# Closing layer 0 by token halves, with the dense branch written ahead of the sparse one

## The reference

```python
m_l = modulate(rmsnorm(h, norm2_w[l]), sh2, sc2)
h = h + g2 * grouped_moe(m_l, router_w, router_bias, ...)      # latent tokens
hc = hc + cg2 * grouped_moe(m_c, router_w, router_bias, ...)   # context tokens, other gates
...
a_l = modulate(rmsnorm(h, norm1_w[l]), sh1, sc1)               # layer 1
a_c = modulate(rmsnorm(hc, norm1_w[l]), csh1, csc1)
q_c, k_c, v_c = project(a_c)                                   # q_c is not used
q_l, k_l, v_l = project(a_l)
```

## Time and profile before

| | |
|---|---|
| median of the runs | 1494.63 us |
| the profiled execution | 1495.13 us, of which the span is 1493.3 us |
| PE busy | 1378.6 us (92% of the span) |
| DVE, ACT, POOL busy | 595.6, 393.9, 153.6 us |
| chain that ended last | PE 72%, SP's queue 10%, DMA 7%, DVE 5% |
| HBM traffic | 325.79 MB read, 14.81 MB written, 228 GB/s over the span |

### The profile page before, as it was taken

The page is one execution under the profiler, slowest core; times in us unless marked ns, Lnnn a source line. Parts: engine busy times, 40 slices in busy tenths (PEclk is TensorE's granted clock), DMA queues, the critical chain, the costliest instruction groups (busy, mean ns, idle before and its releaser), DMA issues.

```text
span 1493.3 us, 29089 instructions
## 1 busy us (share of the span) xinstructions
PE 1378.6 (92%) x12381; PEld 830.0 (56%) x12381; DVE 595.6 (40%) x1095; ACT 393.9 (26%) x970; POOL 153.6 (10%) x182
## 2 busy tenths in 40 slices
PE   5999888999988999998999999998999999998876
PEld 2344444454544588754666666656757776655432
DVE  4365666446454655451222222134264532221112
ACT  2322343443434200321222222104162302221111
POOL 0000113122231300000111111000000001111100
PEclk8999999999999999999999999999999999999998
DMA  8555334333440542416999999892220359999993
GB/s 340 215 172 175 110 138 156 126 117 138 141 142 29 137 117 97 186 59 248 324 389 379 383 380 384 344 367 81 81 104 29 130 221 392 393 394 396 398 402 144
DMA packets 131494, 334.48 MB, mean 224 GB/s; under 512 B 13283, under 2 KB 63259, under 8 KB 125211
## 3 DMA queue, kind: packets, MB, share of 16 engines
q1 hardware_dynamic: 121851, 309.18, 57.0%
q0 software_dynamic: 6208, 12.60, 2.4%
q10 hardware_dynamic: 3296, 10.73, 1.9%
HBM read 325.79 MB, written 14.81 MB: 228 GB/s over the span
## 4 chain that ended last, share of the span: by engine, by line
PE 72%; SPq 10%; DMA 7%; DVE 5%; ACT 2%; issue 2%; ACTq 0%; DVEq 0%; POOLq 0%
PE ps L1592 12%; PE ps L1234 11%; PE ps L1251 7%; SPq L587 7%; PE ps L1485 6%; PE ps L1631 6%; PE ps L1542 5%; PE ps L1178 3%; PE ps L1891 2%; SPq L589 2%; PE ps L1656 2%; PE ps L1803 2%; PE ps L1326 2%; DMA ring<-in_moe_w_down 2%; DMA ssb<-in_moe_w_up 1%
## 5 line engine op out<-in xcount | busy, mean ns | idle before, releaser
L1234 PE MATMUL ps<-aT,ring 128*128 128x512 f32 x384 | 174.8, 603 | 2.2 <-issue 2.2
L1592 PE MATMUL ps<-ring,ssb 128*32 128x256 f32 x2256 | 137.2, 387 | 9.7 <-DMA ring<-in_moe_w_up 8.9
L2415 DVE COPY big<-ps 32x256 f32<-32x256 f32 x162 | 68.6, 423 | 145.9 <-PE ps L1631 144.2
L1592 PE MATMUL ps<-tmp,ssb 128*32 128x256 f32 x1984 | 117.2, 383 | 7.2 <-DMA tmp<-in_moe_w_up 7.2
L2406 DVE TENSOR_TENSOR ssb<-ssb,ps 128x128 f32<-128x128 f32 (+1 forms) x56 | 19.1, 346 | 260.6 <-ACT ssb L1009 259.3
L1234 PEld LDWEIGHTS ps<-aT,ring 128*128 128x128 f32 x384 | 70.6, 191 | 84.8 <-issue 82.6
L1592 PEld LDWEIGHTS ps<-ring,ssb 128*32 128x32 f32 x2256 | 88.1, 112 | 53.0 <-DMA ring<-in_moe_w_up 14.3
L1251 PE MATMUL ps<-aT,ring 128*128 128x512 f32 x256 | 114.2, 595 | 0.0
L1631 PE MATMUL ps<-ring,ssb 128*32 128x256 f32 x1648 | 96.8, 387 | 3.6 <-DMA ring<-in_moe_w_down 2.9
L1592 PEld LDWEIGHTS ps<-tmp,ssb 128*32 128x32 f32 x1984 | 70.4, 111 | 50.2 <-DMA tmp<-in_moe_w_up 9.0
L1022 ACT COPY big<-ps 32x256 f32<-32x256 f32 x162 | 58.7, 363 | 141.4 <-PE ps L1631 139.9
(11 more groups left out here) (434 smaller groups left out, 1944.6 us busy)
## 6 DMA issues: line engine op xcount, KB each, us to landing
ring<-in_ada_w SPq DMA_DIRECT2D x44, 1024.0 KB
ring<-in_moe_w_down SPq DMA_DIRECT2D x40, 1024.0 KB
ring<-in_moe_w_gate SPq DMA_DIRECT2D x56, 512.0 KB
ring<-in_moe_w_up SPq DMA_DIRECT2D x56, 512.0 KB
tmp<-in_moe_w_gate SPq DMA_DIRECT2D x48, 512.0 KB
tmp<-in_moe_w_up SPq DMA_DIRECT2D x48, 512.0 KB
ring<-in_ssd_in_w SPq DMA_DIRECT2D x20, 1024.0 KB
tmp<-in_moe_w_down SPq DMA_DIRECT2D x16, 1024.0 KB
```

The source lines that it names most:

```text
L1234: ins = pe.matmul(ps[:, bank, :], slot(u)[:, k, (i % 2) * P:(i % 2 + 1) * P], aT[:, k, :], start=(k == 0), stop=(k == KD - 1))
L1592: ins = pe.matmul(tiled_gu[32 * c:32 * c + 32, 2 * h + i, :].rearrange("p (r n) -> p r n", r=2), XgT[l][:, k * C + 32 * g:k * C + 32 * g + ...
L2415: ins = dve.tensor_copy(Y[s % 2][32 * g:32 * g + 32, 256 * c:256 * c + 256], tiled_y[32 * c:32 * c + 32, 2 * h + i, :])
```

## The change

Three things are changed.

1. **The end of layer 0 by halves.** `shared_down(b)` now fills bank b with two chunks of one half (bank 0 to 3 latent, 4 to 7 context), by matmuls over 256 tokens. `layer_sum` orders PE's work: banks 0, 1, 2, 3 and 5, the first two tiles of `acc`, bank 6, the mean square of the latent half, banks 7 and 4, the last two tiles. DVE adds the latent half to `hT` (`gated_sum(0)`) between tiles 1 and 2 of `acc`, norms it behind tile 3, and then takes the context half. PE computes the latent keys (`keys(0)`), the mean square of the context half, the first query unit, the context keys (`keys(1)`), and goes on. The rotation of the keys stands behind the second query unit. The root is taken twice (`ROOTS`).
2. **The branches' order.** In PE's and DVE's programs the flag is compared with 1 (`spread`), and the dense branch stands first. The sparse branch is now reached by a jump past the dense code, and falls through into what follows. The other three engines keep `choose`.
3. **SP's queue.** In the sparse case SP waits for all four transfers of pairs before it issues layer 1's first weights. The shared down weights stay ahead of that wait.

```diff
-ROOTS = [1, 2, 1, 1]
+ROOTS = [1, 2, 2, 1]
...
+        def spread(eng, l):
+
+            eng.wait_ge(s_flag, l + 1)
+            return eng.value_load(flag[0:1, 0:1], min_val=0, max_val=1) == 1
...
+                if pairs_used:
+                    for t in range(NT if l == 0 else 0):
+                        sp_.wait_ge(s_yp[0][t], 16)
...
-            norm_modulate(1, 0, T, 0, lambda k: act.wait_ge(s_h2, k + 1))
+            act.wait_ge(s_mod, AMOD_N[1, 0])
+            for h in range(2):
+                part = slice(h * S, (h + 1) * S)
+                for k in range(KD):
+                    act.wait_ge(s_h2, 4 * h + k // 2 + 1)
+                    act.activation(aT[:, k, part], hT[:, k, part], ACT.Square).then_inc(s_sq, 1)
+                act.wait_ge(s_ms, roots_to(2) + h + 1)
+                act.activation(rstd[:, part], ps[:, h, 0:S], ACT.Sqrt, bias=small[:, 15:16]).then_inc(s_rs, 1)
+                for k in range(KD):
+                    act.wait_ge(s_nx, parts_to(2) + KD * h + k + 1)
+                    act.activation(aT[:, k, part], aT[:, k, part], ACT.Identity, bias=mod[:, 1, k, h:h + 1],
+                                   scale=amod[:, 1, 0, k, h:h + 1]).then_inc(s_a, 1)
...
+            def mean_square_half(h):
+                for k in range(KD):
+                    pe.wait_ge(s_sq, squares_to(2) + KD * h + k + 1)
+                    ins = pe.matmul(ps[:, h, 0:S], mean[:, :], aT[:, k, h * S:(h + 1) * S], start=(k == 0), stop=(k == KD - 1))
+                ins.then_inc(s_ms, 1)
...
-                def shared_down(taken):
+                def shared_down(b):
+
+                    h = b // 4
+                    for k in (2 * (b % 4), 2 * (b % 4) + 1):
+                        for f in range(KF):
+                            ins = pe.matmul(ps[:, b, (k % 2) * S:(k % 2 + 1) * S],
+                                            slot(units[f"sd{l}"][f // 2], 2)[:, f % 2, k * P:(k + 1) * P],
+                                            hid[:, f, h * S:(h + 1) * S], start=(k % 2 == 0 and f == 0), stop=False,
+                                            skip_group_check=True)
+                    return ins
+
+                def turn_sum(t):
+
+                    for k in range(KD):
+                        c = (k % 2) * S + (t % 2) * P
+                        ins = pe.matmul(ps[:, 4 * (t // 2) + k // 2, c:c + P], acc[:, t, k * P:(k + 1) * P], ident,
+                                        start=False, stop=(t % 2 == 1), skip_group_check=True)
+                        if t % 2 and k % 2:
+                            ins.then_inc(s_mt, 1)
+
+                def layer_sum(taken, ready):
 
                     for u in units[f"sd{l}"]:
                         arrived(pe, u)
-                    for k in (0, 1, 2, 5, 6, 7, 3, 4):
-                        if k == 3:
-                            taken()
-                        for f in range(KF):
-                            ins = pe.matmul(ps[:, k, 0:n], slot(units[f"sd{l}"][f // 2], 2)[:, f % 2, k * P:(k + 1) * P],
-                                            hid[:, f, 0:n], start=(f == 0), stop=False, skip_group_check=True)
-                    ins.then_inc(s_sd, 1)
+                    for b in (0, 1, 2):
+                        shared_down(b)
+                    taken()
+                    shared_down(3)
+                    shared_down(5)
+                    for t in range(2):
+                        ready(t)
+                        turn_sum(t)
+                    shared_down(6)
+                    mean_square_half(0)
+                    shared_down(7)
+                    shared_down(4).then_inc(s_sd, 1)
+                    for t in range(2, 4):
+                        ready(t)
+                        turn_sum(t)
...
-                sparse = choose(pe, l)
-                with pe.If(sparse):
+                dense = spread(pe, l)
+                with pe.If(dense):
+                    for e in range(1, NE + 1):
+                        for f in range(KF):
+                            hidden_chunk(e, f)
+                        dense_down(e)
+                    pe.wait_ge(s_mr, 16 * (l + 1))
 ...
+                        layer_sum(lambda: None, lambda t: None)
+                with pe.Else():
                     turn_rows(0)
 ...
-                        shared_down(out_taken)
-                        turn_sum(lambda t: pe.wait_ge(s_acc[l], 2 * t + 2))
-                        mean_square(2, T, 0)
 ...
+                        layer_sum(out_taken, lambda t: pe.wait_ge(s_acc[l], 2 * t + 2))
...
-            pe.wait_ge(s_h2, KD)
             arrived(pe, units["k"][0])
-            w = slot(units["k"][0])
-            for h in range(NORM_PARTS[2]):
+
+            def keys(h):
+                w = slot(units["k"][0])
                 part = slice(h * S, (h + 1) * S)
                 for k in range(KD):
                     pe.wait_ge(s_a, parts_to(2) + KD * h + k + 1)
                     for m in range(2):
-                        ins = pe.matmul(ps[:, 4 + m, part], w[:, k, m * P:(m + 1) * P], aT[:, k, part],
+                        ins = pe.matmul(ps[:, 2 + m, part], w[:, k, m * P:(m + 1) * P], aT[:, k, part],
                                         start=(k == 0), stop=(k == KD - 1), skip_group_check=True)
-            ins.then_inc(s_kv, 1)
+                return ins
+
+            keys(0)
+            mean_square_half(1)
...
+                if c == 0:
+                    keys(1).then_inc(s_kv, 1)
+                elif c == 1:
+                    rotate_k()
                 if c:
                     rotate_q(c - 1)
-                else:
-                    rotate_k()
...
+            def gated_sum(q):
+
+                for b in range(4):
+                    dve.wait_ge(s_mt, 4 * q + b + 1)
+                    for k in (2 * b, 2 * b + 1):
+                        h = hT[:, k, q * S:(q + 1) * S]
+                        ins = dve.scalar_tensor_tensor(out=h, in0=ps[:, 4 * q + b, (k % 2) * S:(k % 2 + 1) * S],
+                                                       scalar=mod[:, 0, 40 + k, q:q + 1], in1=h, op0=ALU.mult, op1=ALU.add)
+                    ins.then_inc(s_h2, 1)
...
-                sparse = choose(dve, l)
-                with dve.If(sparse):
+                dense = spread(dve, l)
+                with dve.If(dense):
+                    dve.wait_ge(s_mr, 16 * (l + 1))
+                    dve.memset(acc[:, 0:nt, :], 0.0).then_inc(s_acc[l], 1)
+                    dve.wait_ge(s_acc[l], 1)
+                    for e in range(1, NE + 1):
+                        for f in range(KF):
+                            chunk(e, f)
+                        outputs(e, comb[:, :, e - 1:e])
+                    if l == 0:
+                        gated_sum(0)
+                with dve.Else():
                     rowsT_dve(l, 0)
                     for s in range(NE):
...
+                        if t == 2:
+                            gated_sum(0)
...
-
-            norm(2, T)
+            norm_part(2, 0, T)
+            gated_sum(1)
+            norm_part(2, 1, T)
```

More of the change, by code:

```diff
@@ L1097, in _ @@
             moe_act(0)
[L1099 removed]
+            act.wait_ge(s_mod, AMOD_N[1, 0])
[10 more added lines that the diff above has]
+                                   scale=amod[:, 1, 0, k, h:h + 1]).then_inc(s_a, 1)
             act.wait_ge(s_kv, 1)
             for m in range(2):
[L1103 removed]
+                act.copy(KT[:, m, :], ps[:, 2 + m, :]).then_inc(s_kc, 1)
             for c in range(4):
@@ L1192, in ada_turn @@
                 ins.then_inc(s_b3, 1)
-            def mean_square(i, n, bank):
-                for k in range(KD):
-                    pe.wait_ge(s_sq, squares_to(i) + k + 1)
-                    ins = pe.matmul(ps[:, bank, 0:n], mean[:, :], aT[:, k, 0:n], start=(k == 0), stop=(k == KD - 1))
-                ins.then_inc(s_ms, 1)
             def mean_square_of_result(h):
@@ L1680, in add_dense @@
                               skip_group_check=True).then_inc(s_mt, 1)
-                def turn_sum(ready):
-                    for t in range(nt):
-                        ready(t)
-                        for k in range(KD):
-                            ins = pe.matmul(ps[:, k, t * P:(t + 1) * P], acc[:, t, k * P:(k + 1) * P], ident,
-                                            start=False, stop=(t == nt - 1), skip_group_check=True)
-                            if t == nt - 1:
-                                ins.then_inc(s_mt, 1)
                 C = max(RANK_ROWS[l])
```

41 lines of the change are left out of this document (8 added, 33 removed).

## The result

The changed kernel took **1485.81 us** (median of 10 runs, 1478.55 to 1490.82), the kernel before 1494.55 (10 runs beside it, 1489.93 to 1502.41). The ratio is 0.9947, 95% interval [0.9929, 0.9966]: 7.9 us less by that ratio, between 5.1 and 10.6 (the medians differ by 8.7). Two later comparisons gave 0.9943 and 0.9946. The sign was right; about half of the gain was not foreseen.

What follows compares the result with a forecast made beforehand. PE was taken to bound layer 0's end, with bare waits such as 3.81 us before the keys. 1495.13 - 6.7 (halves) + 2.7 (entry) = 1491.1 us for a profile, 1490.6 against the median; range 1488.0 to 1495.0.

Steps and rivals of the forecast that it cites:

- The end by halves: Layer 0's end, shared product through both halves' keys: PE needs 55.4 us instead of 62.15, a gain of 6.7 us.
- The pairs: Layer 0's end: with SP's wait the scatter ends some 2 us sooner, and PE does not wait for the tiles.
- PE's jump at layer 0's entry: PE's taken branch at layer 0's experts: 3.5 us, covered by more than 9 us before the rows are copied.
- The entry term: Layer 0's experts' entry: DVE's jump of 5.6 us makes PE start 3.2 us late, 2.7 us lost after 0.5 comes back.
- upper bound of 5.5 us: Layer 0's entry: the most that DVE's jump could lose, with the queues of weights deeper than at 1000.0.
- The half microsecond given back: Layer 0's experts: of the 3.2 us lost at the entry, 0.5 comes back where PE later waits for a down weight.
- full rate would be 13.8, so 1.9 us go to the restart: Layer 0's keys behind the norm's gap: 64 instructions take 15.74 us, 1.9 us of it the restart that the halves can win.
- The free jump: Rival, layer 0's entry: DVE's jump costs 0 to 0.6 us, giving 1488.2 us; chance 0.12.
- The late pairs: Rival, layer 0's end: transfers come no sooner, PE stands 3.7 us for tile 1, giving 1494.3 us; chance 0.10.
- the dear jump: Rival, layer 0's entry: 5.5 us late, giving 1493.4 us, or 1494.4 with layer 1 beyond its slack; chance 0.15.
- a second fetch in layer 1: From the slower rival: DVE fetches twice at both entries, layer 1 losing 4 us and layer 0 8; 1499.9 us, chance 0.08.
- while PE's queue is full; I count nothing: Layer 0's end: the new branches behind the last combine and last tile cost 0.5 us each, counted as nothing.

Runs made afterwards that it cites:

- late_entry: The changed kernel with five more unused reciprocals on DVE between its jump and its copy of the first expert's rows, layer 0 only: 1493.75 us, ratio 1.0022.
- before_again: The kernel before once more, unchanged, for a second profile and the spread of its times: 1492.28 us, ratio 0.9997.
- order_only: The kernel before with only the order of the branches exchanged in PE's and DVE's programs: 1492.58 us, ratio 0.9991.
- no_sp_wait: The changed kernel without SP's wait for the pairs, layer 1's first weights issued as their slots come free: 1489.79 us, ratio 0.9983.
- dve_dense_first: The changed kernel with the sparse branch first again in PE's program, the dense one first in DVE's alone: 1495.20 us, ratio 1.0013.
- halves_only: The changed kernel, SP's wait included, with the sparse branch first again in PE's and DVE's programs: 1491.63 us, ratio 0.9981.

## Why the prediction was wrong

**What held.** The end by halves: 55.56 us for 55.4. The pairs: the transfers started 6.6 us behind the shared product (8.7 before; the forecast had counted 2 us less), and PE waited for nothing. SP's wait cost no one anything. PE's jump at layer 0's entry was hidden, although it took 6.78 us and not 3.5. So was DVE's in layer 1: the copy came 2.1 us behind the branch, where it waited for the transposes, as it had 2.5 us behind it before.

**The entry term**, 2.7 us lost, had the right mechanism and nearly the right size. Its upper bound of 5.5 us followed from no row; the longest jump of DVE in any trace, 6.70 us, would make it 4.3. DVE's jumps took 3.47, 5.73 and 5.44 us in the three traces of the changed kernel, where one row had given 5.6. PE was 2.5 us late in the mean (7.09 against 4.59 for the kernel before), the timed comparison says 2.2. The half microsecond given back did not show in `late_entry`.

**The step that failed** is the clock, in two places. The first is "full rate would be 13.8, so 1.9 us go to the restart". The row was right for its execution. But the end took 93.05 us there, 96.46 in `before_again`, 93.59 in `order_only`, whose PE does the same work at this place without the long jumps, and 86.63 in every trace of the changed kernel. The mean is 94.4, a gain of 7.7 us instead of 6.4 (93.05 - 86.63). The timeline of `before_again` has a second slow group, the mean square, which took 7.13 in the earlier trace rows and has a granted clock of 0.81 here:

```profile
997.28 7.31 PE L1686 MATMUL ps<-c,big 128*128 128x128 f32 x64
1006.92 8.83 PE L1197 MATMUL ps<-aT,mean 128*128 128x512 f32 x16 [2.33 <-ACT aT L831]
1019.56 15.74 PE L1784 MATMUL ps<-aT,ring 128*128 128x256 f32 x64 [3.81 <-ACT aT L840]
```

The wait for the first squares is 2.33 us there and was 0.62; the change closes both waits. So of the 3.4 us between the two traces half is this wait and half the clock. The wait has DVE's jump in it, 6.1 us from its branch to its next instruction there: in `order_only`, where this jump is gone, PE does not wait for the squares. Its keys, behind the same 3.81 us of idle time, take 3.0 us more than the full rate, at a granted clock of 0.83, where the forecast counted 1.9:

```profile
1003.46 7.13 PE L1202 MATMUL ps<-aT,mean 128*128 128x512 f32 x16
1014.41 16.83 PE L1788 MATMUL ps<-aT,ring 128*128 128x256 f32 x64 [3.81 <-ACT aT L845]
```

The second place is what was left out: the price of the clock was read from one stage of one execution, while the rest of the program has half-clock stretches too, and they do not fall alike in every execution. Over all runs with a recorded clock PE spends 72.6 us at half clock in the kernel before (127 runs) and 62.8 in the changed one (34 runs). The 9.8 us are worth up to 4.9 us of time. The forecast's 1.9 us stand for 3.8 of them. The other 6 us of half clock, or 3 us of time, together with the entry's 0.5, cover most of the 3.9 us between -4.0 and -7.9; the remainder is within the interval (5.1 to 10.6). How much of it belongs to the end (1.3 us by the traces' mean, the longer wait and the clock together) and how much to the stretches elsewhere, the attention's among them, the runs do not settle.

**The rivals.** The free jump (1488.2) was nearest by its number, and for the wrong reason: the entry wasn't free. The late pairs are what `no_sp_wait` showed. Neither the dear jump nor a second fetch in layer 1 came, though `dve_dense_first` had a DVE jump of 6.70 us.

**The branches' order** was weighed as a price at the entry only. What it brings stood in the prediction as half a sentence, "while PE's queue is full; I count nothing". That was right for the changed kernel, but left out that without it the halves bring next to nothing (`halves_only`). A taken branch past the dense code lasted 3.3 to 7.0 us on PE in all traces, a fall-through 87 or 88 ns. The Trainium skill, Advanced Engine Details and Errata, section Control Flow Timing, gives about 108 ns for a compare-and-branch; on PE only the fall-throughs are near that. Its page Runtime: NRT & Kernel Launch, section Instruction fetch mechanics, tells of a wait for a fetch behind a taken branch whose target isn't at hand; the 4.64 us of "issue" in `halves_only` agree. No run here tests that it is this fetch, nor why the same jump takes 3.5 us in some kernels and 6.6 in others.

## What to carry to other kernels

Before closing a gap, ask what else lies in it: here a jump of PE did (3.5 us in the kernel before, 6.6 once the halves had closed the gap), and it had to be moved to a place with cover in the same change. Put a long taken branch where its engine still has queued work, for each engine on its own: PE's belonged at the entry, DVE's at the end. And count a gap at more than its width: the clock behind it is part of the price, and it is read from several executions, not from one.

## What the runs showed of the hardware

- A taken branch over the dense code took PE 3.3 to 3.9 us at some places and 6.3 to 7.0 at others. At layer 0's end it took 3.5 and 3.7 us in the two traces of the kernel before and 6.6 in `halves_only` and `dve_dense_first`. DVE's next instruction came 3.4 to 6.7 us behind its branch in layer 0, and 1.8 to 3.1 in layer 1, where that is no longer than the wait for its data.
- The granted clock's low stretches differ from one execution to the next in parts of the program whose code is the same. Layer 0's shared hidden chunks, which stand ahead of all that was changed, took 71.1 us in some traces and 72.8 in others. The runs of one kernel spread over 8 to 21 us, and their times follow the mean clock: the correlation was -0.88 over 127 runs of the kernel before, 11.6 us for 0.01 by a straight line (15 were expected).
- Matmuls whose result nobody reads, put where PE waits, kept the clock up: keys of 7.15 us instead of 8.83 (granted clock 1.00 against 0.80), and a gate-and-up product of 5.39 instead of 6.68 to 7.47.
